# PEER stage of a two-block transformer: every fourth expert row of the first two token tiles is added by VectorE in SBUF instead of by TensorE in PSUM

## The reference, cut to what matters

```python
def chunk(xc):                                   # 128 tokens x 1024
    q = (xc @ w_pq).reshape(P_CHUNK, P_HEADS, 2, P_DK // 2)
    s = jnp.einsum('thpd,hpkd->thpk', q, sub_keys)
    s_top, i_top = lax.top_k(s, P_TOPK)
    ...
    best, ci = lax.top_k(cand.reshape(P_CHUNK, P_HEADS, P_TOPK * P_TOPK), P_TOPK)
    ...
    gate = jax.nn.softmax(best.astype(jnp.float32), axis=-1).astype(xc.dtype)
    act = jax.nn.gelu(jnp.einsum('thkd,td->thk', u_tab[expert], xc), approximate=False)
    return jnp.einsum('thk,thkd->td', gate * act, v_tab[expert])
x = x + g2 * peer_ffn(h2, ...)                   # 512 tokens, then rms_norm
```

## Time and profile before

| | |
|---|---|
| median of 3 runs | 2996.41 us (2990.37 to 2997.92) |
| the profiled execution | 2993.21 us, of which the traced span is 2991.9 us |
| mean granted TensorE clock | 0.968 of full speed |
| TensorE matmul busy | 2631.4 us (88% of the span) |
| VectorE busy | 1573.2 us (53%) |
| ScalarE busy | 652.1 us (22%) |
| GpSimd busy | 547.9 us (18%) |
| DMA of the gathers (software queue) | 536.90 MB in 73728 packets |

### The profile page before, as it was taken

One profiled execution on the slowest core, in us unless ns is written; L12 is line 12 of the kernel. 1 busy time (PEld: TensorE's weight loads), 2 busy tenths in 40 slices (PEclk: granted clock), 3 DMA queues, 4 the chain that ended last, 5 costly groups with the idle time before them and its releaser, 6 DMA issues.

```text
span 2991.9 us, 23372 instructions
## 1 busy us (share of the span) xinstructions
PE 2631.4 (88%) x8074; PEld 1386.7 (46%) x8074; DVE 1573.2 (53%) x3510; ACT 652.1 (22%) x1573; POOL 547.9 (18%) x523
## 2 busy tenths in 40 slices
PE   8998899999999999999989988879877777777776
PEld 4684446666444444466657533435332323232222
DVE  1106335443106992366524677657575676758554
ACT  2114220001002002266411112222121221222111
POOL 0000000000000000000001333444444434444332
PEclk9997899999999999999989999999999999999999
DMA  3220023343212221000126999999999999999997
GB/s 138 99 85 1 22 85 141 141 168 118 101 72 93 84 79 50 14 1 29 50 119 266 390 373 388 404 398 406 397 415 415 391 420 420 420 420 420 420 420 311
DMA packets 87300, 686.95 MB, mean 230 GB/s; under 512 B 9976, under 2 KB 10616, under 8 KB 12816
## 3 DMA queue, kind: packets, MB, share of 16 engines
q0 software_dynamic: 73728, 536.90, 44.1%
q1 hardware_dynamic: 11408, 143.53, 12.6%
q10 hardware_dynamic: 2048, 5.03, 0.5%
HBM read 683.32 MB, written 2.10 MB: 229 GB/s over the span
## 4 chain that ended last, share of the span: by engine, by line
PE 64%; DMA 24%; DVE 7%; ACT 3%; issue 1%; POOL 0%; ACTq 0%; DVEq 0%
PE psum L345 34%; DMA slot<-in_experts,expert 12%; PE psum L908 12%; DMA weights<-in_experts,expert 12%; PE psum L841 3%; PE psum L750 3%; PE psum L702 2%; DVE slot L1847 2%; PE psum L808 2%; PE psum L772 1%; PE psum L823 1%; DVE weights L1847 1%; PE psum L758 1%; ACT spare_row L1304 1%; PE psum L519 0%
## 5 line engine op out<-in xcount | busy, mean ns | idle before, releaser
L908 PE MATMUL psum<-slot,spare_row 128*128 128x512 f32 x1096 | 515.0, 614 | 127.2 <-ACT spare_row L1304 125.1
L908 PE MATMUL psum<-weights,spare_row 128*128 128x512 f32 x952 | 454.1, 622 | 151.9 <-ACT spare_row L1304 145.6
L1847 DVE CUSTOM_DVE_ANT_0 slot<-slot,hT 128x1024 f32<-128x1024 f32 x274 | 333.6, 1223 | 191.3 <-DMA slot<-in_experts,expert 189.6
L345 PE MATMUL psum<-xnT,weights 128*128 128x257 f32 (+2 forms) x1568 | 423.9, 432 | 2.8 <-DVE xnT L1353 2.8
L908 PEld LDWEIGHTS psum<-slot,spare_row 128*128 128x128 f32 x1096 | 204.9, 194 | 414.5 <-issue 206.9
L1847 DVE CUSTOM_DVE_ANT_0 weights<-weights,hT 128x1024 f32<-128x1024 f32 x238 | 290.0, 1223 | 187.0 <-DMA weights<-in_experts,expert 186.2
L1901 POOL DMA_INDIRECT weights<-in_experts,expert x238 | 250.5, 1053 | 751.3 <-PE psum L908 392.7
L1901 POOL DMA_INDIRECT slot<-in_experts,expert x274 | 294.3, 1074 | 422.1 <-PE psum L908 407.9
L908 PEld LDWEIGHTS psum<-weights,spare_row 128*128 128x128 f32 x952 | 179.2, 197 | 414.1 <-ACT spare_row L1304 215.0
L345 PEld LDWEIGHTS psum<-xnT,weights 128*128 128x128 f32 x1568 | 298.8, 191 | 118.5 <-issue 82.2
L1299 ACT ACTIVATE coef<-hidden 128x2 f32<-128x2 f32 (+1 forms) x257 | 52.3, 204 | 1000.2 <-DVE hidden L1847 1000.2
(11 more groups left out here) (320 smaller groups left out, 2532.9 us busy)
## 6 DMA issues: line engine op xcount, KB each, us to landing
weights<-in_w_mod SPq DMA_DIRECT2D x12, 2048.0 KB, 8.6
weights<-in_w_up SPq DMA_DIRECT2D x11, 2048.0 KB, 7.7
weights<-in_w_in SPq DMA_DIRECT2D x8, 2048.0 KB, 8.7
weights<-in_w_pq SPq DMA_DIRECT2D x8, 2048.0 KB, 12.1
weights<-in_w_out SPq DMA_DIRECT2D x6, 2048.0 KB, 8.3
weights<-in_w_in_t SPq DMA_DIRECT2D x4, 2048.0 KB, 13.5
weights<-in_w_down SPq DMA_DIRECT2D x4, 2048.0 KB, 8.1
weights<-in_w_o_mla SPq DMA_DIRECT2D x4, 2048.0 KB, 8.7
```

Of the source, the lines that this page charges most:

```text
L345: last = pe.matmul(out, lhsT, rhs, start=start and n == 0, stop=stop and n == len(pairs) - 1)
L908: last = pe.matmul(acc.pair[:, half, :], k.diags[pick % 8], k.slots[slot][:, D + half * 512:D + (half + 1) * 512], start=h0 == 0 and j == ...
L1847: ins = dve.tensor_tensor_reduce(slot[:, 0:D], slot[:, 0:D], k.h2[:, i, :], 1.0, 0.0, ALU.mult, ALU.add, hid[:, j:j + 1])
```

## The change

Of the first 256 picks those with number 3, 7, 11, ... (64 picks, 32 for each tile, always the second of a pair) go another way. TensorE leaves out their matmuls and ScalarE their diagonals. VectorE adds coefficient times row to a sum of 128 x 1024 numbers that lies in SBUF (`vector_sum`, in columns of `sig_a` that are free by then), behind the steps that follow the pair: one `tensor_scalar` for the first of a tile, `scalar_tensor_tensor` for the 31 others. A new semaphore `added` counts them, and GpSimd waits for it before it loads such a slot again. `finish_tile` of the first two tiles adds the PSUM pair and this sum in its first operation, and multiplies by `g2` in one more.

```diff
--- before.py
+++ after.py
@@ -160,6 +160,22 @@
 
     def picks_before(self, b):
         return sum(self.picks(n) for n in range(b))
+
+    def added(self, pick):
+
+        return pick < 2 * PH * TOPK and pick % 4 == 3
+
+    def tensor_picks(self, n):
+
+        return n - min(n, 2 * PH * TOPK) // 4
+
+    def used(self, pick):
+
+        n = self.tensor_picks(pick + 1)
+        return (self.sem.added, pick + 1 - n) if self.added(pick) else (self.sem.picked, n)
+
+    def vector_sum(self, i):
+        return self.sig_a[:, 4 * i:4 * i + 4, 0:2 * P]
 
     def groups(self, b):
 
@@ -902,11 +918,16 @@
             for g, (j0, size) in enumerate(k.groups(b)):
                 for j in range(j0, j0 + size):
                     slot, loads, before = k.gathers[pick]
-                    pe.wait_ge(s.diag, pick + 1)
+                    if k.added(pick):
+                        pick += 1
+                        continue
+                    n = k.tensor_picks(pick)
+                    final = j == nh * TOPK - 1 or k.added(pick + 1) and j == nh * TOPK - 2
+                    pe.wait_ge(s.diag, n + 1)
                     pe.wait_ge(s.ld_slot[slot], 16 * loads)
                     for half in range(2):
-                        last = pe.matmul(acc.pair[:, half, :], k.diags[pick % 8], k.slots[slot][:, D + half * 512:D + (half + 1) * 512],
-                                         start=h0 == 0 and j == 0, stop=last_batch and j == nh * TOPK - 1)
+                        last = pe.matmul(acc.pair[:, half, :], k.diags[n % 8], k.slots[slot][:, D + half * 512:D + (half + 1) * 512],
+                                         start=h0 == 0 and j == 0, stop=last_batch and final)
                     last.then_inc(s.picked)
                     pick += 1
                 if g == k.route_begins(b) and b + 1 < len(k.order):
@@ -1299,9 +1320,11 @@
                 act.activation(cf[:, j0:j0 + size], hid[:, j0:j0 + size], ACT.Gelu).then_inc(s.gelu)
                 act.wait_ge(s.coef, group)
                 for j in range(j0, j0 + size):
-                    if pick > 7:
-                        act.wait_ge(s.picked, pick - 7)
-                    act.activation(k.diags[pick % 8], k.ident[:], ACT.Copy, scale=cf[:, j:j + 1]).then_inc(s.diag)
+                    n = k.tensor_picks(pick)
+                    if n > 7 and not k.added(pick):
+                        act.wait_ge(s.picked, n - 7)
+                    if not k.added(pick):
+                        act.activation(k.diags[n % 8], k.ident[:], ACT.Copy, scale=cf[:, j:j + 1]).then_inc(s.diag)
                     pick += 1
                 for _ in range(k.steps(b)):
                     next(beside, None)
@@ -1786,7 +1809,7 @@
         dve.wait_ge(*done)
         yield from top16(nh, lambda r: cand_rows[:, r, :], lambda r: rest_rows[:, r, :], best, besti)
         if b > 1:
-            dve.wait_ge(s.picked, k.picks_before(b - 1))
+            dve.wait_ge(s.picked, k.tensor_picks(k.picks_before(b - 1)))
         dve.tensor_tensor(g, best, best[:, :, 0:1].to_broadcast([P, nh, TOPK]), ALU.subtract).then_inc(s.gate_logits)
         dve.tensor_scalar(flat(part[:, 0]), flat(besti), 4, None, ALU.logical_shift_right).then_inc(v.up())
         dve.tensor_scalar(flat(part[:, 1]), flat(besti), 15, None, ALU.bitwise_and).then_inc(v.up())
@@ -1820,10 +1843,19 @@
 
     def finish_tile(i):
         y, u = k.h2[:, i, :], of["peer", i]
-        dve.wait_ge(s.picked, (i + 1) * PH * TOPK)
-        dve.tensor_tensor(halves(y), u.pair, halves(k.g2), ALU.mult).then_inc(u.out)
-        yield
-        dve.wait_ge(*u.free)
+        dve.wait_ge(s.picked, k.tensor_picks((i + 1) * PH * TOPK))
+        if i < 2:
+            dve.wait_ge(s.added, (i + 1) * PH * TOPK // 4)
+            dve.tensor_tensor(y.rearrange("p (a n) -> p a n", a=4), u.pair.rearrange("p a (b n) -> p (a b) n", b=2), k.vector_sum(i), ALU.add).then_inc(u.out)
+            yield
+            dve.wait_ge(*u.free)
+            dve.tensor_tensor(y, y, k.g2, ALU.mult).then_inc(v.up())
+            done = v.now()
+        else:
+            dve.tensor_tensor(halves(y), u.pair, halves(k.g2), ALU.mult).then_inc(u.out)
+            done = u.free
+            yield
+        dve.wait_ge(*done)
         dve.tensor_tensor(k.x[:, i, :], k.x[:, i, :], y, ALU.add).then_inc(s.x5)
         yield
         r = inverse(P, i, ("last", i))
@@ -1854,10 +1886,23 @@
                 for _ in range(k.steps(b)):
                     next(beside, None)
                 next(late, None)
+                for j in range(j0, j0 + size):
+                    if k.added(pick - size + j - j0):
+                        add_row(pick - size + j - j0, i, cf[:, j:j + 1], group)
             for _ in beside:
                 pass
         for _ in finish_tile(NT - 1):
             pass
+
+    def add_row(pick, i, scale, group):
+        sum_, n = k.vector_sum(i), k.used(pick)[1]
+        row = k.slots[k.gathers[pick][0]][:, D:2 * D].rearrange("p (a n) -> p a n", a=4)
+        dve.wait_ge(s.coef, group)
+        if pick % (PH * TOPK) == 3:
+            dve.tensor_scalar(sum_, row, scale, None, ALU.mult).then_inc(s.added)
+        else:
+            dve.wait_ge(s.added, n - 1)
+            dve.scalar_tensor_tensor(sum_, row, scale, sum_, ALU.mult, ALU.add).then_inc(s.added)
 
     norm1()
     in_projection()
@@ -1893,7 +1938,7 @@
         for j in range(nh * TOPK):
             slot, loads, before = k.gathers[pick]
             if before is not None:
-                pool.wait_ge(s.picked, before + 1)
+                pool.wait_ge(*k.used(before))
             elif slot == 0:
                 pool.wait_ge(*of["out2", 0, 0].full[-1])
             elif slot > 5 and slot % 2 == 0:
@@ -1957,7 +2002,7 @@
 SINGLE = """act_step dve_step ones ld_meta ld_const ld_mixer ld_diag ld_ctx ld_final1 ld_rope2 ld_norm2 ld_sub ld_count ld_final2
 root xn1 forget run rqk causal16 ret_masked ret_sq ret_mixed fox_nm fox_exp fox_p xn2 mod_sum silu_c conv3 up_silu gain1 ctxn x3 xn3
 down_read pad conv centred ln_sq ln_scaled ln_silu kr feature_sq feature kr_copied a_nm a_p q_rope merged spread gain2 x4 h2
-gate_logits gate_exp gated expert hidden gelu coef diag picked x5 y st_out""".split()
+gate_logits gate_exp gated expert hidden gelu coef diag picked added x5 y st_out""".split()
 SEVERAL = dict(ld_x=NT, ld_weights=3, ld_rope1=2, ld_slot=10, psum_full=8, psum_out=8)
 
 
```

## The result

The changed kernel takes 3019.84 us in the median of 4 runs (3012.2 to 3022.05) against 2996.76 us for the kernel before: a ratio of 1.0075, with an interval from 1.0059 to 1.009. That is 23 us slower; the prediction was 3001 and its range ended at 3012.

A forecast was written before the change was run, and what follows sets the result against it. DMA at 420 GB/s was taken as the bound, with slots freed late by TensorE or VectorE. Terms +11.1 (additions), -2.5 and -5.1 (TensorE relief), +1 (clock) gave +4.5 us on 2996.4: 3001 us, range 2986 to 3012.

The forecast's parts named there:

- The base and VectorE's 11.1 us: DMA at 420 GB/s sets the pace; additions cost +2.7, +4.8, +3.6 us in pairs 1-9, 19-25, 37-41.
- TensorE's -2.5 and -5.1 us: Relieved TensorE gives back 2.5 us in the 16 pairs from 2030.8 us and 5.1 in four dense-step stretches.
- What it gives back on TensorE: Prediction's section on stretches with dense steps: their excess over DMA's pace partly comes back, -2.5 and -5.1 us.
- The granted clock at +1 us: Pairs 86 to 127, without dense steps: longer TensorE gaps make slow pairs common; bounds 0 and about 7, taken +1 us.
- costs nothing while a gather has slack: Pairs without dense steps: a slot 1.7 us later is free of cost, as a gather's slack is near 2.5 us.
- if pairs 86 to 127 slow down: Stated sign of a wrong prediction: these pairs, without dense steps, were expected to stay 4.99 us apart.
- Where a slow pair and a long routing step meet, some tenths are lost: Stretch without dense steps: the only loss seen from slow TensorE pairs, within the +1 us taken for the clock.
- It is not later than before in any stretch: Release of an added pick's slot, behind the steps plus 1.20 us: no later than before, so no loss booked.
- TensorE was what counted: Rival, chance 0.20: TensorE's full 4.0 and 10.2 us come back, additions cost half of 11.1; about 2986 us.
- The lower clock takes hold: Rival, chance 0.13: TensorE stays at 1.2 GHz in the 42 pairs from 2114.6 us, 7 us more; about 3011.
- The additions cost in full: Rival, chance 0.12: 12 bare additions cost 14.4 us and TensorE's gains are cut to nothing; 3011 us.
- The operation is dearer: Rival, chance 0.03: each VectorE addition takes 2.4 us, twice as long; the 12 places cost 25.5 us; about 3030.

The follow-up runs named there:

- e3: Kernel before with VectorE's additions put on top, TensorE and ScalarE still doing all picks, slot free when both are done: 3006.74 us, ratio 1.0038.
- e1: Changed kernel with each addition cut to 4 of its 1024 columns, TensorE still skipping the 64 picks: 2996.62 us, ratio 1.0003 to the kernel before.
- e2: Changed kernel with constant-data matmuls on TensorE in place of 62 of the 64 skipped picks, additions kept: 3008.12 us, ratio 1.0047 to the kernel before.
- e8: Changed kernel with constant-data matmuls in place of skipped picks from pick 151 on alone (26 picks): 3006.25 us, ratio 1.0047 to the kernel before.
- e5: Changed kernel with additions cut to 4 columns and constant-data matmuls for 62 of the 64 skipped picks: 2990.85 us, ratio 0.9984 to the kernel before.
- e4: Kernel before with the change made in the second tile alone (picks 131 to 255, 32 additions): 3013.36 us, ratio 1.0058.
- e6: Changed kernel with the addition right behind the coefficient, ahead of the pair's routing and dense steps: 3017.01 us, ratio 1.0074 to the kernel before.

## Why the prediction was wrong

The terms of the sum can be set against the profile by stretches of pairs: what was booked (with half of each excess of a dense stretch), and the difference to the kernel before in the changed kernel, in e3 (additions at TensorE's full load) and in e1 (relief with tiny additions). All are us, of single executions.

| pairs | booked | changed | e3 | e1 |
|---|---|---|---|---|
| 1 to 17 | +2.1 | -0.4 | +2.3 | -2.6 |
| 17 to 35 | +3.9 | +5.2 | +4.4 | +0.8 |
| 35 to 46 | +3.6 | +4.9 | +4.6 | +2.6 |
| 46 to 70 | -3.7 | +0.5 | +0.3 | +2.6 |
| 70 to 86 | -2.5 | +4.7 | +1.7 | -1.4 |
| 86 to 128 | +1 | +13.3 | -0.2 | +6.5 |

**The base and VectorE's 11.1 us: right.** DMA at 420 GB/s is the pace, tiles 2 and 3 did not move, and the operation takes 1.28 us. e3, which adds VectorE's work and leaves TensorE's, lost 11 us by the medians, and where it was booked: 2.7, 4.8 and 3.6 us were booked for the batches with routing, and e3's stretches there are longer by 2.3, 4.4 and 4.6. e2 puts the additions at 14 us. One reading of the earlier trace rows was off: the first weight load does not lie in the second stretch alone but half in the first (1.44 and 1.21 MB). And the number holds only for additions at a full clock, as the second half shows.

**TensorE's -2.5 and -5.1 us: wrong.** This is the first step that failed. "What it gives back on TensorE" counted 7.6 us from the excess of stretches over DMA's pace, and the runs show about 0 in its place. The ratios of e2 and e8, which differ by this relief alone up to pair 75, are both 1.0047, each within 0.17%; I estimate that this leaves room for some 7 us either way. The stretches point to nothing as well: from pair 1 to 86 it is 492.6 us with the relief against 492.3 without it where the additions are tiny (e1 and e5), and 505.5 against 504.5 where they are full (changed and e2). In pairs 70 to 86, where TensorE was busy for 82.34 of 83.80 us, e1 takes 82.4 us with it relieved and e5 takes 82.0 with it at its load. Only the bound of 0 was right. What the excess came from is not shown. Nor do the runs say whether the relief would be worth something at an equal clock, since it also brought the clock of the first half down from 0.95 to 0.90 (e5 to e1). In pairs 70 to 86 the booking on VectorE failed too: eight additions, 9.6 us, were to vanish in 11.6 us of waits for DMA. The changed kernel still waits 9.3 us for DMA there, and the stretch grew by 4.7 us instead.

**The granted clock at +1 us: wrong in size.** This is the second and larger step. The mechanism was the one named: gaps of about 3 us behind the single picks, slow pairs after them, slots late. It was priced as something that "costs nothing while a gather has slack". In place of 1 us the runs show 8 us (e2 and e8 against the changed kernel, 0.28%), or 6 us with tiny additions (e1 against e5, 0.19%); both figures are what is left after anything that the relief gives back. The prediction's own sign for this came true: it was to be wrong "if pairs 86 to 127 slow down", and they did, by 13.3 us up to pair 128. "Where a slow pair and a long routing step meet, some tenths are lost" was the sentence that should have been worked out. In pairs 98 to 114, which have the routing steps, the additions alone cost 1.5 us (e3), the low clock with tiny additions 1.9 (e1), and both 8.8; e4 and e6 repeat that with +8.5 and +9.3. My reading is that slack was counted for each cause by itself, though a slow pair and a late addition draw on the same 6 slots: GpSimd's longest wait for TensorE in this stretch is 2.6 us in e3, 4.2 in e1 and 6.2 in the changed kernel. No run varied the number of slots, so this last link is argued and not shown.

**How it adds up.** By the medians the additions with TensorE at its load cost 14 us (e2) where 11.1 were booked, and taking the load away costs 8 to 9 more where -7.6 and +1 were booked. That is the 23 us.

**"It is not later than before in any stretch": no loss by the release's place.** e6, with the release ahead of the steps, changed nothing. e5, which has the earlier releases and neither the addition's time nor the lower clock, is 5 us under the kernel before; that this is the freer slots is likely, but no run isolates it.

**The rivals.** "TensorE was what counted" is refuted by the direction of the change, and e1, without the time of the additions, shows none of its 14 us. "The lower clock takes hold" was right in its place and its price of about 7 us, though not in its condition: TensorE did not stay at 1.2 GHz but was granted either level by turns (a mean of 0.85 in pairs 86 to 128), and was idle in between. "The additions cost in full" was near as well, 14.4 us against the 11 and 14 of e3 and e2. They were set up as alternatives with 3011 us each; nothing in the profile made them exclude each other, and both came. "The operation is dearer" is refuted by the 1278 ns. The Trainium skill's rule that a scalar_tensor_tensor with two non-bf16 sources in SBUF runs at half the throughput (Vector Engine (DVE) Microarchitecture Reference, section Points that are easy to get wrong) does not show as the prediction read it: the operation takes hardly more than the 1222 ns of a reduce of the same size. Against the `tensor_scalar` with one source, 740 ns, it does take 1.7 times as long, and which of the two the rule is meant against no run decides. Its warning of gaps that throttle TensorE (TensorE: Matmul & The Clock Gate, section HAM oscillation — how this bites in real kernels) does show: clocks of 0.83 to 0.91 from pair 70 on after the gaps grew, 0.98 and 1.00 in pairs 98 to 114 when they were filled (e2 and e8).

What stays open: why the additions cost 0.63% against e5 but only 0.38% against the kernel before (e3), whether the two losses act together over the whole program as they seem to behind pair 86, and what the relief of TensorE would be worth at an equal clock.

## What to carry to other kernels

An engine that looks full need not be the one that counts: here TensorE was busy for 82.34 of 83.80 us, and taking a quarter of its picks away did not make that stretch shorter than leaving its load on. To price a relief, ask what the stretch will wait for next. Where TensorE already has idle gaps between bursts, taking matmuls out can slow those that are left, and slower matmuls hold buffers longer: here useless matmuls made the program 8 us faster. Several small delays on one ring of buffers should be priced together against one slack, not each against all of it. And when a profile is cut into stretches, look whether a load has moved over a cut before two neighbours are read as a loss and a gain.

## What was not expected of the hardware

A `scalar_tensor_tensor` cut from 1024 to 4 columns still took 0.22 us in e1 (median 222 ns), so that the 62 tiny ones are 14 us of VectorE time; they cost nothing that showed. The clock fell for gaps of no more than 3 us: in pairs 98 to 114 of e1 TensorE's longest wait for a diagonal is 3.0 us and the clock is 0.88. In the kernel before the longest is 2.1 us there and the clock 0.98, in e2 2.4 us and also 0.98.
